# Differential attention in a two-block forward pass: the mixed probabilities turned by VectorE and a trip through DRAM, the first map's division moved to the head norm

## The reference

```python
# diff_attend: per head, two softmax maps, subtracted
p1 = softmax(q1 @ k1.T / sqrt(64)); p2 = softmax(q2 @ k2.T / sqrt(64))
o  = (p1 - lam * p2) @ v                 # 128 value columns per head
# diff_head_out
y_a = o * rsqrt(mean(o * o) + 1e-6) * subln * (1 - lam_init)
```

## Time and profile before

| | |
|---|---|
| runs (3) | 1902.48, 1902.87, 1903.45 us; median 1902.87 |
| profiled execution, first to last instruction (span) | 1899.9 us |
| mean granted clock of TensorE, share of full speed | 0.997 |
| PE busy | 1874.5 us, 99% |
| DVE busy | 1337.0 us, 70% |
| ACT busy | 1004.9 us, 53% |
| DMA | 375.17 MB, 197 GB/s over the span |

### The profile page before, as it was taken

One profiled execution on the slowest core, in us unless ns is written; L12 is line 12 of the kernel. 1 busy time (PEld: TensorE's weight loads), 2 busy tenths in 40 slices (PEclk: granted clock), 3 DMA queues, 4 the chain that ended last, 5 costly groups with the idle time before them and its releaser, 6 DMA issues.

```text
span 1899.9 us, 26256 instructions
## 1 busy us (share of the span) xinstructions
PE 1874.5 (99%) x10688; PEld 1587.0 (84%) x10688; DVE 1337.0 (70%) x1826; ACT 1004.9 (53%) x1462; POOL 39.0 (2%) x47
## 2 busy tenths in 40 slices
PE   7999999999999999999999999999999999999998
PEld 3899888999888998988788887788888888778887
DVE  5788789888789878855755566755566555786555
ACT  3465544564544655444544456554455444666444
POOL 1300000000000000000000000000000000000000
PEclk9999999999999999999999999999999999999999
DMA  9645675535676644465567754367755776536775
GB/s 364 223 147 182 222 241 195 188 124 174 221 246 198 211 156 134 155 220 187 161 219 225 225 190 144 133 210 220 228 197 181 226 226 213 182 111 197 226 230 166
DMA packets 123319, 375.17 MB, mean 197 GB/s; under 512 B 14080, under 2 KB 32640, under 8 KB 122432
## 3 DMA queue, kind: packets, MB, share of 16 engines
q1 hardware_dynamic: 118320, 352.11, 56.0%
q0 software_dynamic: 4592, 19.90, 3.0%
q10 hardware_dynamic: 288, 1.51, 0.2%
HBM read 360.87 MB, written 10.49 MB: 195 GB/s over the span
## 4 chain that ended last, share of the span: by engine, by line
PE 92%; DVE 5%; ACT 1%; DMA 1%; issue 1%; SPq 0%; DVEq 0%; ACTq 0%
PE PS L676 28%; PE PS L678 27%; PE PS L677 27%; DVE w_lo L2110 2%; PE PS L850 1%; PE PS L869 1%; DMA raw<-weights 1%; PE PS L1258 1%; ACT w_hi L1512 1%; PE PS L1091 1%; PE PS L959 1%; PE PS L1247 1%; PE PS L940 1%; PE PS L859 0%; PE PS L813 0%
## 5 line engine op out<-in xcount | busy, mean ns | idle before, releaser
L2110 DVE TENSOR_TENSOR w_lo<-raw,w_hi 128x1024 fp32r<-128x1024 f32 x600 | 731.7, 1233 | 390.9 <-ACT w_hi L1512 389.4
L1512 ACT ACTIVATE w_hi<-raw 128x1024 fp32r<-128x1024 f32 x600 | 625.3, 1057 | 446.9 <-DMA raw<-weights 443.9
L676 PE MATMUL PS<-w_hi,h_hi 128*128 128x512 f32 (+1 forms) x1280 | 494.9, 387 | 2.1 <-DVE w_lo L2110 1.3
L678 PE MATMUL PS<-w_hi,h_lo 128*128 128x512 f32 (+1 forms) x1280 | 488.4, 382 | 0.0
L677 PE MATMUL PS<-w_lo,h_hi 128*128 128x512 f32 (+1 forms) x1280 | 488.1, 381 | 0.0
L676 PEld LDWEIGHTS PS<-w_hi,h_hi 128*128 128x128 f32 x1280 | 240.7, 188 | 54.8 <-issue 5.1
L678 PEld LDWEIGHTS PS<-w_hi,h_lo 128*128 128x128 f32 x1280 | 240.7, 188 | 47.2
L677 PEld LDWEIGHTS PS<-w_lo,h_hi 128*128 128x128 f32 x1280 | 240.9, 188 | 45.5 <-issue 1.0
L676 PE MATMUL PS<-h_hi,w_hi 128*128 128x256 f32 x896 | 258.3, 288 | 0.7 <-issue 0.3
L676 PE MATMUL PS<-w_hi,g_hi 128*128 128x512 f32 (+1 forms) x656 | 257.1, 392 | 0.1
L677 PE MATMUL PS<-h_lo,w_hi 128*128 128x256 f32 x896 | 253.4, 283 | 0.0
(11 more groups left out here) (302 smaller groups left out, 1663.8 us busy)
## 6 DMA issues: line engine op xcount, KB each, us to landing
raw<-weights SPq DMA_DIRECT2D x610, 512.0 KB, 3.9
act_mem<-arena SPq DMA_DIRECT2D x144, 64.0 KB, 3.0
arena<-act_mem SPq DMA_DIRECT2D x36, 256.0 KB, 3.6
qk<-weights POOLq DMA_DIRECT2D x12, 512.0 KB, 4.2
v<-weights POOLq DMA_DIRECT2D x12, 512.0 KB, 5.1
x<-weights SPq DMA_DIRECT2D x8, 512.0 KB, 8.0
qk<-cond_in POOLq DMA_DIRECT2D x2, 1024.0 KB, 5.1
arena<-arena SPq DMA_DIRECT2D x32, 64.0 KB, 2.6
```

What stands on the lines that cost most here:

```text
L676: pe.matmul(dst, hi, m_hi_, start=first, stop=False, **kw)
L678: return pe.matmul(dst, lo, m_hi_, start=False, stop=last, **kw)
L1512: nc.scalar.activation(w_hi[:, r, :], raw[:, r, :], ACT.Copy).then_inc(w_hi_ready, 1)
L2110: V.tensor_tensor(w_lo[:, r, :], raw[:, r, :], f32(w_hi[:, r, :]), ALU.subtract).then_inc(w_lo_ready, 1)
```

## The change

The mixed probabilities no longer go through PE and ACT. DVE transposes their 32x32 blocks into `mixw_s` (two buffers); the output is so ordered that for each query the g key tiles lie side by side (g is 2 in pass 0, 4 in passes 1 and 2). SP stores them to `mix_mem` in DRAM with four transfers and reads them back with one into `mixw_t`, which holds for each key the order (query, tile). `values` takes tile j as every g-th element of a row: the stationary operand is read with a step of 8 bytes in pass 0 and of 16 bytes in passes 1 and 2. The stores of unit n stand in SP's list behind the load of slot c+5, the read behind that of slot c+6, where c is the first slot of step n's pair. In pass 0 a contiguous piece has 256 bytes, in passes 1 and 2 512 bytes.

The division by the first map's sum is left out: what is mixed is `p1' - lam * s1 / s2 * p2'` with the undivided maps, a factor s1 too large. All s1 are kept (`den_first`), and the head norm takes epsilon times s1 squared in place of epsilon, so that the factor drops out there. For this DVE gets two small instructions at the end of the eight units (`head_means`), the second behind a wait for the last of ACT's squares and ahead of `spectrum_bias`.

Two semaphores of POOL's gate row become one.

```diff
-        mixw_t = scratch(3584, 2048).rearrange("p (b k t) -> p b k t", b=2, k=4)
+        mixw_s = scratch(1024, 1024).rearrange("p (b n) -> p b n", b=2)
+        mixw_t = scratch(3584, 2048).rearrange("p (b q n) -> p b q n", b=2, q=2)
...
+            def mix_out(p, n):
+                u, nt = 8 * p + n, len(key_tiles(p))
+                sp.wait_ge(mix_blocks, u + 1)
+                if u >= 2:
+                    sp.wait_ge(mix_moved[u % 2], 16 * (u // 2))
+                for i in range(4):
+                    rows = mixw_s[32 * i:32 * i + 32, n % 2, 0:nt * P].rearrange("p (j e) -> p j e", j=4)
+                    sp.dma_start(mix_mem[u % 2, :, :, i, 0:32 * nt].rearrange("j a e -> a j e"), rows).then_inc(mix_stored, 16)
+            def mix_in(p, n):
+                u, nt = 8 * p + n, len(key_tiles(p))
+                h, qt = n // 2, n % 2
+                sp.wait_ge(mix_stored, 64 * (u + 1))
+                if n >= 4:
+                    sp.wait_ge(pv_done, u - 3)
+                dst = mixw_t[:, h % 2, qt, 0:nt * P].rearrange("p (i e) -> p i e", i=4)
+                sp.dma_start(dst, mix_mem[u % 2, :, :, :, 0:32 * nt].rearrange("j a i e -> (j a) i e")).then_inc(mix_moved[u % 2], 16)
+            mix_moves = {start[f"pass{p}"] + part["v"] + 2 + 2 * n + RING: (p, n) for p in range(3) for n in range(8)}
+            mix_returns = {c + 1: u for c, u in mix_moves.items()}
...
-            def turn(p, n):
-                pe.wait_ge(mixw_ready, 8 * p + n + 1)
-                if n >= 1:
-                    pe.wait_ge(mixw_t_ready, 8 * p + n)
-                for j in range(len(key_tiles(p))):
-                    mm = pe.transpose(PS[:, TURN, j * P:(j + 1) * P], mixw[:, j * P:(j + 1) * P], const("ident"))
-                mm.then_inc(turned, 1)
...
-                pe.wait_ge(mixw_t_ready, 8 * p + n + 1)
+                pe.wait_ge(mix_moved[u % 2], 16 * (u // 2 + 1))
+                by_keys = mixw_t[:, h % 2, qt, 0:len(kt) * P].rearrange("p (t g) -> p g t", g=len(kt))
...
-                    mm = pe.matmul(PS[:, HEADS_OUT + qt, h * P:(h + 1) * P], mixw_t[:, h % 2, j, qt * P:(qt + 1) * P],
+                    mm = pe.matmul(PS[:, HEADS_OUT + qt, h * P:(h + 1) * P], by_keys[:, j, :],
...
-                nc.scalar.activation(head_rt, head_ss, ACT.Sqrt, scale=1.0 / P,
-                                     bias=eps[:, 0:1]).then_inc(head_rt_ready, 1)
+                act.wait_ge(head_ms_ready, p + 1)
+                nc.scalar.activation(head_rt, head_ss, ACT.Sqrt).then_inc(head_rt_ready, 1)
...
-                    take_turned(p, n)
...
-                link(V.reciprocal(rden[:, 0:2], den[:, 0:2]))
-                V.tensor_tensor(wden[:, 0:1], rden[:, 1:2], neg_lam[:, LAYER_OF[p], :], ALU.mult)
-                link(V.tensor_scalar(mixw[:, 0:nk], probs[:, 0, 0:nk], rden[:, 0:1], None, ALU.mult))
-                V.scalar_tensor_tensor(mixw[:, 0:nk], probs[:, 1, 0:nk], wden[:, 0:1], mixw[:, 0:nk], ALU.mult,
-                                       ALU.add).then_inc(mixw_ready, 1)
+                link(V.reciprocal(rden_second, den_second))
+                link(V.scalar_tensor_tensor(wden[:, 0:1], rden_second, neg_lam[:, LAYER_OF[p], :], den_first[:, i:i + 1], ALU.mult,
+                                            ALU.mult))
+                link(V.scalar_tensor_tensor(mixw[:, 0:nk], probs[:, 1, 0:nk], wden[:, 0:1], probs[:, 0, 0:nk], ALU.mult, ALU.add))
+                if u >= 2:
+                    dve.wait_ge(mix_stored, 64 * (u - 1))
+                g = len(key_tiles(p))
+                V.transpose(mixw_s[:, n % 2, 0:nk].rearrange("p (j e g) -> p g j e", j=4, g=g),
+                            mixw[:, 0:nk].rearrange("p (g j e) -> p g j e", g=g, j=4)).then_inc(mix_blocks, 1)
+            def head_means(p):
+                link(V.scalar_tensor_tensor(head_eps, den_first, EPS, den_first, ALU.mult, ALU.mult))
+                dve.wait_ge(head_sq, p + 1)
+                V.scalar_tensor_tensor(head_ss, head_ss, 1.0 / P, head_eps, ALU.mult, ALU.add).then_inc(head_ms_ready, 1)
...
                 splits(c0 + part["gu"] + 2)
+                head_means(p)
                 if p != 1:
                     spectrum_bias(l)
```

More of the change, by code:

```diff
@@ L269, in build @@
         act_mem = nc.dram_tensor("act_mem", (4, 32, 4, P), F32, kind="Internal").ap()
+        mix_mem = nc.dram_tensor("mix_mem", (2, 4, 32, 4, P), F32, kind="Internal").ap()
         gate_mem = nc.dram_tensor("gate_mem", (1, D), F32, kind="Internal").ap()
@@ L311, in build @@
         rden = stat[:, 24:32]
+        den_first = den[:, 0:8]
+        den_second = rden[:, 0:1]
+        rden_second = rden[:, 1:2]
         head_ss = stat[:, 32:40]
+        head_eps = mx[:, 0:8]
         head_rt = stat[:, 40:48]
@@ L398, in build @@
         p_ready = sem("p_ready")
-        mixw_ready = sem("mixw_ready")
-        turned = sem("turned")
-        mixw_t_ready = sem("mixw_t_ready")
+        mix_blocks = sem("mix_blocks")
+        mix_stored = sem("mix_stored")
+        mix_moved = [sem(f"mix_moved{j}") for j in range(2)]
         pv_done = sem("pv_done")
         head_sq = sem("head_sq")
+        head_ms_ready = sem("head_ms_ready")
         head_rt_ready = sem("head_rt_ready")
@@ L429, in build @@
         tail_loaded = sem("tail_loaded")
-        gate_stored = sem("gate_stored")
-        gate_loaded = sem("gate_loaded")
+        gate_moved = sem("gate_moved")
         out_done = sem("out_done")
@@ L595, in load @@
                     swap_halves(swaps[n])
+                if n in mix_moves:
+                    mix_out(*mix_moves[n])
+                if n in mix_returns:
+                    mix_in(*mix_returns[n])
                 if n in moves:
@@ L664, in _ @@
             pool.wait_ge(gated_ready, 18)
[L665 to L668, removed]
+            pool.dma_start(gate_mem.rearrange("o (p k) -> p (o k)", p=P), gate_cols).then_inc(gate_moved, 16)
+            pool.wait_ge(gate_moved, 16)
+            pool.dma_start(gate_row, gate_mem.to_broadcast([P, D])).then_inc(gate_moved, 16)
+            pool.wait_ge(gate_moved, 32)
             pool.dma_start(layer[:, 0:ntail], tail_in).then_inc(tail_loaded, 16)
@@ L852, in scores @@
                 mm.then_inc(sc_done, 1)
-            def turn(p, n):
-                pe.wait_ge(mixw_ready, 8 * p + n + 1)
-                if n >= 1:
-                    pe.wait_ge(mixw_t_ready, 8 * p + n)
-                for j in range(len(key_tiles(p))):
-                    mm = pe.transpose(PS[:, TURN, j * P:(j + 1) * P], mixw[:, j * P:(j + 1) * P], const("ident"))
-                mm.then_inc(turned, 1)
             def values(p, n):
                 h, qt = n // 2, n % 2
-                pe.wait_ge(mixw_t_ready, 8 * p + n + 1)
+                kt = key_tiles(p)
+                u = 8 * p + n
+                pe.wait_ge(mix_moved[u % 2], 16 * (u // 2 + 1))
                 if n == 0:
                     pe.wait_ge(*taken(p, 5))
-                kt = key_tiles(p)
+                by_keys = mixw_t[:, h % 2, qt, 0:len(kt) * P].rearrange("p (t g) -> p g t", g=len(kt))
                 for j, t in enumerate(kt):
-                    mm = pe.matmul(PS[:, HEADS_OUT + qt, h * P:(h + 1) * P], mixw_t[:, h % 2, j, qt * P:(qt + 1) * P],
+                    mm = pe.matmul(PS[:, HEADS_OUT + qt, h * P:(h + 1) * P], by_keys[:, j, :],
                                    v[:, t, h * P:(h + 1) * P], start=(j == 0), stop=(j == len(kt) - 1))
@@ L921, in run_pass @@
                         values(p, n - 1)
-                    turn(p, n)
                 pe.wait_ge(*taken(p, 11))
@@ L1627, in exps @@
                 act.wait_ge(nm_ready, 8 * p + n + 1)
-                for m in range(2):
+                i = 2 * (n // 2) + n % 2
+                for m, total in enumerate((den_first[:, i:i + 1], den_second)):
                     ins = nc.scalar.activation(probs[:, m, 0:nk], PS[:, SCORES + m, 0:nk], ACT.Exp,
                                                bias=neg_max[:, m:m + 1], scale=SUB ** -0.5,
-                                               accum_out=den[:, m:m + 1])
+                                               accum_out=total)
                 ins.then_inc(p_ready, 1)
@@ L1640, in head_squares @@
                 if n == 7:
-                    link(ins)
+                    ins.then_inc(head_sq, 1)
             def taps(p, j):
@@ L1653, in taps @@
                 ins.then_inc(tap_ready, 1)
[L1655 to L1661, removed]
             def rope_copy(n, bank, c):
@@ L2290, in softmax_mix @@
                 nk = P * len(key_tiles(p))
+                u, i = 8 * p + n, 2 * (n // 2) + n % 2
                 dve.wait_ge(p_ready, 8 * p + n + 1)
-                link(V.reciprocal(rden[:, 0:2], den[:, 0:2]))
-                V.tensor_tensor(wden[:, 0:1], rden[:, 1:2], neg_lam[:, LAYER_OF[p], :], ALU.mult)
-                link(V.tensor_scalar(mixw[:, 0:nk], probs[:, 0, 0:nk], rden[:, 0:1], None, ALU.mult))
```

(6 more changed lines are left out.)

## The result

| | before | after |
|---|---|---|
| median of 6 runs | 1903.16 us (1902.44 to 1905.26) | 1915.47 us (1912.26 to 1918.88) |
| ratio, 95% interval | | 1.006 [1.0049, 1.007] |
| span of the profiled execution | 1899.9 us | 1910.0 us |
| mean granted clock of TensorE | 0.997 | 0.997 |

What follows compares the result with a forecast made beforehand. PE was taken as the bound (99% busy). Transposes -8.8 and the stepped stationary operand +14.5 gave +5.7, less a few tenths +5.5, so 1902.87 + 5.5 = 1908.4 us; whole range 1894.5 to 1911.5.

Steps and rivals of the forecast that it cites:

- the sign: Whole kernel: slower was given a chance of 0.45, faster 0.36, same 0.19.
- the trip's term: Store to DRAM and read back before values: in time by 1.1 us, last unit covered by longer values; 0 us.
- the column price: PE's extra time per stepped column of the values' weight loads, taken from DVE's row L2539: 0.89 ns.
- Transposes leave PE: Attention on PE: 80 transposes at 0.11 us each go away, 8.8 us less.
- The stationary operand: Values' weight loads, 16-byte step in passes 1 and 2: 0.113 us more per record, 128 records, 14.5 us; pass 0 nothing.
- Less a few tenths because the first load of each group runs under the matmul before: Discount on the sum of +5.7 us for the values' first weight loads, giving +5.5 us.
- DVE, hidden: DVE in an attention step: 0.39 to 0.84 us more work, fitting in its 1.50 us of idle time less 0.44.
- Head norm, 0: DVE's 0.2 us instruction hides under ACT's table load; later spectrum_bias just hidden, 0 to 0.3 us in passes 0 and 2.
- rival B: Values' weight loads: half the price, 0.06 us per record, +7 - 8.8 = -1.8, 1901 us; chance 0.15 together with D.
- A: Values' weight loads: PE reads the 16-byte step at full pace, -7.8 with last-unit stalls, 1895.1 us; chance 0.36.
- C: DRAM trip late in every step, 0.3 us 14 times, 4 us on top of A; chance 0.07.
- D: The change does nothing, pointless for PE; under 0.02, counted with B at 0.15.

Runs made afterwards that it cites:

- e6_runs: The changed kernel with plain layout: tiles one behind the other, no step on PE, stores in pieces of 128 bytes; 1898.24 us, ratio 0.997.
- pairs alone: The changed kernel with its tiles interleaved in twos, step 8 bytes in every pass, DVE's order as in the change; 1896.38 us, ratio 0.9961.
- the first unit in between: The changed kernel with tiles interleaved in twos and the first unit's softmax_mix between the fourth rope_turn and the split (passes 1, 2); 1897.71 us, ratio 0.997.
- the change again: The changed kernel once more, unchanged, five rounds; 1914.33 us, ratio 1.0054 against the kernel before.
- e7_runs_early: The plain-layout version of the changed kernel, with the first unit's softmax_mix ahead of the fourth rope_turn in passes 1 and 2; 1899.38 us, ratio 0.9978.
- e5_pairs: The changed kernel with only the interleaving altered, tiles in twos, so PE steps by 8 bytes in every pass; 1896.38 us, ratio 0.9961.
- e2_step16: The kernel before, PE's transposes kept, with only the stationary operand's step added (16 bytes in passes 1 and 2, 8 in pass 0); 1918.49 us, ratio 1.0081.
- e2_step32: The kernel before, PE's transposes kept, with the stationary operand read in steps of 32 bytes in all passes; 1923.46 us, ratio 1.0105.

## Why the prediction was wrong

Its main mechanism and its sign were right, the sign with a stated chance of only 0.45. The step that failed is the trip's term, put at 0: the first unit of each pass was not looked at. Besides, the column price was set a little low, and the range was too narrow.

*Transposes leave PE, -8.8.* Measured -8.6, with the values of pass 0 in it. Right.

*The stationary operand, +14.5.* "DVE's row is the only one with a wide step" was the right row to take: DVE's 0.89 ns per column against 0.97 / 8 = 0.121 us per record, 0.95 ns per column, on PE. 15.5 us, 1.0 more. That a price from another engine, read at 32 bytes, would hold for PE at 16 was argued and not shown, so that it came out within 7% is in part luck. The nothing that the sum took for pass 0's 8 bytes is shown by no row of before, which has no load with a step; in the change such a load took 197 ns against 191, and a unit of pass 0 0.47 us against 0.44, nearly nothing. The forecast of 1.8 us values, loads near 300 ns and a step of 8.8 us stands in the trace as 1.86, 329 and 8.88.

*"Less a few tenths because the first load of each group runs under the matmul before."* No such discount: all eight records pay, 8 x 0.121 = 0.97. 0.2 us.

*The trip, 0.* The step that failed. It was worked out for a middle unit and for the last, and **never for the first unit of a pass**, where the rotation and a split stand ahead of the mix in DVE's list and PE reaches the values sooner. The prediction's own times for the trip would have shown it. In the trace of before, DVE's reciprocal of that unit starts at 369.05 in pass 1, so blocks at 370.9, read landed 4.1 + 3.6 later at 378.6; the values start there at 378.39, and without the transposes 0.44 sooner: 0.7 us late. Measured, in PE's starts: 0.4, 0.8 and 0.7 us in passes 0, 1 and 2, 2.0 in all, with the row of PE waiting for `mix_mem` that the prediction had named as a sign against itself. That the trip itself was 1.0 us shorter than reckoned was made up for by DVE's stepped write (1.13 us, the upper of the two prices named) and a longer landing (4.0). In the other units the trip is in time, and in the last the long values cover it, both as forecast (in pass 2 with 0.1 us to spare, and 0.07 lost); e6_runs shows the other half, a last unit that waits once the values are short.

*DVE, hidden.* Right: 1.17 us of idle time are left. The chain of small results took 2.19 us, within 1.84 to 2.29.

*Head norm, 0.* Right, by ACT's table load of 1.28 us between its last square and its root (at 150.59 us in the trace of before, at 149.39 in that of the change), by the start of L966 and by the run of that part alone: ratio 0.9999 [0.999, 1.0008].

*What is left.* 1.2 us lie in small shifts, nearly all outside attention. The largest lies between 1000 and 1200 us: 0.5 in the first trace of the change, 0.4 in the second, none in pairs alone, 1.1 with the first unit in between. The chain of the first trace of the change shows what it is:

```profile
1131.62 4.94 DMA raw<-weights
...
1142.31 0.44 DVE arena L2749
1142.74 0.04 issue
```

A weight load lands late, ACT's and DVE's lists follow it, and PE waits behind them. The same load took 3.2 us in the trace of before and 4.9 in both traces of the change; with the first unit in between it is another load, of 5.7 us (4.3 before). Why they land late, and the smaller shifts, stay open.

So by the trace: 5.5 forecast, +1.2 for the columns, +2.0 for the first units, +0.2 for the transposes, +0.1 for a last unit, +1.2 of shifts: 10.1 with rounding. By medians it was 12.3, and 11 when the second set of five is added (median of all eleven 1914.5, against 1903.5). The rest of the miss is the spread of executions. All later ones took 2.1 to 2.3 us more than their span, so the trace of before belongs to one of some 1902.1 us, an estimate, 1.1 under its median, and that of the change lies 3.2 under its own: 10.1 - 1.1 + 3.2 = 12.2. Single executions of the kernel before lie between 1900.5 and 1907.1 us. What moves them is not shown, as there is one trace of it. In the two traces of the change it is the waits for weights at the start. Over the sixteen executions of before in the set of the change again, the longer ones have the lower mean granted clock of TensorE, 0.999 at 1901.4 us and 0.995 at 1907.1 (1 is full speed; in the trace of before the clock reads 0.50 from 20 to 24 us and 1.00 from 26 to 1890), so the clock may have a part in it. Three runs within 1 us of each other had made the median look firmer than it is. The upper end of the range, 1911.5, had only 2 to 3 us for everything that was not in the sum.

Two readings in the prediction were loose, and nothing hangs on them. PE's waits behind the longest one add up to 9.9 us in the trace of before, not to a few, though PE has no idle time in the attention stretches of passes 1 and 2. And 0.06 us x 128 records is 7.7 us, so rival B's time was 1901.8 and not 1901.

*The rivals.* A (full pace) falls with the 329 ns, but e6_runs with its 1898.2 shows what it priced: 1895.1 plus the waits at the first units that it left out, 1.7 us by PE's starts; the other 1.4 are within the spread of executions. B (half price) falls: a record costs 0.121 us more, not 0.06. C (trip late every step) falls with 1.0 us or more to spare in every middle unit. D falls: the transposes were worth their 8.6 us.

## What to carry to other kernels

When work is moved off the bounding engine, look at the step with which that engine must read what comes back: 8.6 us of transposes were traded for 15.5 us of slower weight loads, and interleaving by two instead of four keeps the gain (197 ns a load instead of 329, 1896.4 us). When a result takes a longer way, work out its time for the first and the last turn of each loop as well as for a middle one; the orders of the lists around them are others. Where an instruction is moved forward in an engine's list, ask what it will wait for there, since all behind it in the list waits too: 0.92 us at DVE's reciprocal in e7_runs_early.

## What the runs showed of the hardware

A weight load of 128 fp32 columns takes 192 ns contiguous (e6_runs), 197 with a step of 8 bytes (e5_pairs), 329 with 16 (the change, e2_step16) and 334 with 32 (e2_step32). Writes pay the same way, of which the rows of before had shown nothing. DVE's transpose of 128x512 took 712 ns writing contiguously (e6_runs), 714 with a step of 8 bytes (e5_pairs) and 1128 with 16 (the change):

```profile
L2318 DVE STREAM_TRANSPOSE arena<-arena 128x512 f32<-128x512 f32 x16 | 18.0, 1128 | 0.6
```

ACT's copy of 128x512 from PSUM took 598 ns contiguous (before), 1095 with 16 (e2_step16) and 1113 with 32 (e2_step32). A store of 64 KB in pieces of 128 bytes lands in 2.1 us (e6_runs) where one in pieces of 256 takes 1.9 (e5_pairs) and one in pieces of 512 takes 1.8 (the change), as medians.
